# Attention in batches of two pairs of heads: where scores, turns and values stand between the weight chunks

## The chip, the cores and the metric

The kernel runs on one core of one Trainium2 chip. The metric is the device time of one execution in microseconds (us), and of several runs the median. The engines are named as in the profile: PE is TensorE (PEld is its loading of weights), DVE is VectorE, ACT is ScalarE, POOL is GpSimd, and SP's queue issues the loads of weights.

## The reference

The program is a stack of transformer layers over 256 tokens of width 1024: two layers of a first kind, then four of a second kind. The change touches only the attention of the second kind, which stands in three places: mixer "a" (layers 0 and 3) and mixer "c" (layer 2). Layer 1 has a mixer without attention. Everything is computed in 32-bit floats.

```python
def second_block(x, ...):                      # cut
    for i in range(4):
        x = x + 0.5 * rms_norm_2(swiglu(rms_norm_2(x, g[0]), ...), g[1])
        h = rms_norm_2(x, g[2])
        m = (mixer_a, mixer_b, mixer_c)[i % 3](h, ...)
        x = x + rms_norm_2(m, g[3])
        x = x + 0.5 * rms_norm_2(swiglu(rms_norm_2(x, g[4]), ...), g[5])

# mixer_a: 16 heads of width 64; a band of 64-token chunks, with a learned bias by distance
    s = einsum('bqhd,bkhd->bhqk', qc, kb) * scale + bias
    p = softmax(where(valid, s, NEG_INF));  o = einsum('bhqk,bkhd->bqhd', p, vb);  return o @ w_o
# mixer_c: 8 heads, each with two score maps of width 64 and values of width 128
    s = einsum('bqhmd,bkhmd->bmhqk', qblk, k) * scale + alibi
    p = softmax(where(allowed, s, NEG_INF)); a = p[:, 0] - lam_full * p[:, 1]
    o = einsum('bhqk,bkhe->bqhe', a, v);  return (rms_norm_2(o, subln_g) * (1 - lambda_init)) @ w_o
```

## The kernel before

**Products in three parts.** Weights arrive from memory in chunks of 1 MB (128 partitions by 2048 numbers). ACT rounds a chunk to `whi` (`Scalar.split`, shown as L1315 `whi<-raw`), DVE takes the rest to `wlo` (L1899 `wlo<-raw,whi`), and PE multiplies `whi`, `wlo` with the activations, which are split in the same way. So a product is three matmuls. Five chunks have room at once (`SLOTS`), and the split that stands at step c is that of chunk c+3 (`AHEAD`). SP loads chunk c once PE is done with chunk c-5.

**An attention stage** has 12 chunks for the queries, keys and values (`ATTEND`: v v q k q k q k q k v v) of 48 matmuls each, and then 4 blocks of the output weights. The last three blocks are multiplied in `edge`, for one half of one tile of tokens after the other. The product of a chunk goes to one of three PSUM banks in turn (0, 1, 2), and DVE takes it out with the factor of the norm (L2138 for q and k, L2142 for v).

**The eight pairs.** The heads are worked on in eight pairs, b = 0 to 7 (in "c" a pair is one head with its two maps). Each pair has the same steps: PE makes the scores (`scores`, L998 and L1000), DVE adds the bias and finds the maximum (`mask`, L2320), ACT takes the exponentials (`exps`), DVE multiplies by the reciprocals of the sums (`weigh`, L2328 and L2333; in "c" L2337 to L2343, which also mix the two maps), PE transposes the probabilities (`turn_probs`, L1013), ACT copies them out of PSUM (`keep_turned`, `prob_t<-ps`), PE multiplies them with the values (`values`, L1031 and L1033; in "c" L1025 to L1027), and DVE keeps the result (`keep_out`, L2357; in "c" L2354, after ACT's squares for the norm, `square_out`). `prob` and `prob_t` have two buffers, for even and odd b. Scores stand in banks 4 and 5, transposed probabilities in 6 and 7, and the result of one pair in bank 3.

**The order** is written out by hand, and all engines walk it in step: the scores of pairs 0, 2, 4, 6 stand in the middle of chunks 5, 7, 9, 11, those of pairs 1, 3, 5, 7 at the end of the same chunks. A pair is turned at the end of the next chunk (even b) or the one after it (odd b), and its values come one chunk later. The values of pairs 5, 6, 7 and the turns of 6 and 7 come after chunk 11, in `attend_end`. There, in "a", three of the four quarters of the first output block (`out_part`, L911 `whi,hi_first`: 6 matmuls each) fill the gaps. The fourth quarter has to wait for bank 3, so it comes when pair 7 has been kept. Output block n of "a" takes the features of pairs 2n and 2n+1, which ACT and DVE split as well (`pairs_hi`, `pairs_lo`, L2186). In "c" the result is normed first (POOL finds the factor, `scale_out` L2376 applies it), transposed by PE (`turn_attended`, L653) and split (`spot_hi`, `spot_lo` L2104). The transposes of the first half stand between the values of pairs 5 and 6.

The kernel's functions that the change touches follow.

## Time and profile before

| What | us |
| --- | --- |
| median of three runs | 2595.43 |
| the three runs | 2595.39, 2599.72, 2595.43 |
| span of the profiled execution, first to last instruction | 2589.7 |
| median of the runs less that span | 5.7 |
| PE busy | 2560.5 (99%) |
| DVE busy | 1687.8 (65%) |
| ACT busy | 1322.3 (51%) |
| share of the mean 16 DMA engines in the large queue | 58.0% |

The profiled execution has no time of its own beside the span; the runs are shown as they were timed. The granted clock of PE is 0.999 of full speed over the span. A matmul of 256 columns is listed with some 0.28 us, but one starts 0.117 us after the other, so starts are to be compared, not durations. Idle time that a row shows in brackets ends at that start and begins at the modelled end of the matmul ahead.

### The profile page before, as it was taken

Reading aid. Unit: us, or ns where it says so; the run is one execution under the profiler, and the core shown is the slowest. Engines: PE = TensorE matmul, PEld = TensorE weight load, DVE = VectorE, ACT = ScalarE, POOL = GpSimd, SP = SyncE. Lnnn points to the kernel's source line nnn. Section 1 sums busy time; section 2 is a strip of 40 time slices with the busy share of each in tenths; the row PEclk is TensorE's granted clock in tenths of the full one; section 3 lists DMA queues with packets and bytes.
Section 4 is the critical chain, followed back from the end, with each engine's and each line's share of the span. In section 5 each row is a group of like instructions: output and inputs, shape, how many; then the busy total and the mean of one; then the engine's idle time right before and its main releaser. Section 6 shows DMA issues by size and latency. Waiting matters only on the chain.

```text
span 2589.7 us, 43298 instructions
## 1 busy us (share of the span) xinstructions
PE 2560.5 (99%) x18489; PEld 2376.5 (92%) x18489; DVE 1687.8 (65%) x2365; ACT 1322.3 (51%) x1938; POOL 158.0 (6%) x228
## 2 busy tenths in 40 slices
PE   9999999999999999999999999999999999999998
PEld 8999898998998989989988998998899899897997
DVE  7778577885664766656556765656776566566663
ACT  7766376663543554444455444444554354355542
POOL 2110011000000000000011000002000000000000
PEclk9999999999999999999999999999999999999999
DMA  7267452764766546666665766756467566563863
GB/s 227 95 182 209 158 163 82 196 195 158 209 195 207 176 131 194 189 179 193 190 212 149 200 184 183 196 182 195 142 159 192 193 178 191 196 202 100 217 189 120
DMA packets 568313, 460.26 MB, mean 178 GB/s; under 512 B 10298, under 2 KB 529290, under 8 KB 568122
## 3 DMA queue, kind: packets, MB, share of 16 engines
q1 hardware_dynamic: 562615, 441.91, 58.0%
q0 software_dynamic: 4656, 15.30, 1.8%
q8 instruction: 146, 2.39, 0.4%
q14 instruction: 45, 0.37, 0.0%
q10 hardware_dynamic: 851, 0.28, 0.0%
HBM read 456.37 MB, written 1.10 MB: 177 GB/s over the span
## 4 chain that ended last, share of the span: by engine, by line
PE 90%; DVE 5%; ACT 3%; DMA 1%; issue 1%; POOL 0%; SPq 0%; DVEq 0%; POOLq 0%; ACTq 0%
PE ps L911 28%; PE ps L776 16%; PE ps L778 16%; PE ps L777 16%; PE ps L730 3%; PE ps L732 3%; PE ps L731 3%; DVE wlo L1899 1%; ACT h_hi L1315 1%; PE ps L653 1%; ACT prob L1315 1%; DVE h_lo L1961 1%; ACT whi L1315 1%; DMA raw<-in_w_in 1%; PE ps L1013 1%
## 5 line engine op out<-in xcount | busy, mean ns | idle before, releaser
L1899 DVE TENSOR_TENSOR wlo<-raw,whi 128x2048 fp32r<-128x2048 f32 (+1 forms) x419 | 957.4, 2287 | 495.4 <-ACT whi L1315 495.1
L1315 ACT ACTIVATE whi<-raw 128x2048 fp32r<-128x2048 f32 (+2 forms) x421 | 802.7, 1910 | 790.2 <-DMA raw<-in_ff_w_in 418.1
L776 PE MATMUL ps<-h_hi,whi 128*128 128x256 f32 x3584 | 1005.7, 281 | 0.0
L778 PE MATMUL ps<-h_hi,wlo 128*128 128x256 f32 x3584 | 1002.5, 280 | 0.0
L777 PE MATMUL ps<-h_lo,whi 128*128 128x256 f32 x3584 | 1001.8, 280 | 0.0
L776 PEld LDWEIGHTS ps<-h_hi,whi 128*128 128x128 f32 x3584 | 673.9, 188 | 5.0 <-issue 5.0
L778 PEld LDWEIGHTS ps<-h_hi,wlo 128*128 128x128 f32 x3584 | 674.4, 188 | 0.0
L777 PEld LDWEIGHTS ps<-h_lo,whi 128*128 128x128 f32 x3584 | 673.5, 188 | 0.0
L911 PE MATMUL ps<-whi,hid_lo 128*128 128x512 f32 x880 | 296.3, 396 | 0.0
L911 PE MATMUL ps<-whi,hid_hi 128*128 128x512 f32 x880 | 295.4, 394 | 0.0
L911 PE MATMUL ps<-wlo,hid_hi 128*128 128x512 f32 x880 | 294.6, 394 | 0.0
L730 PE MATMUL ps<-whi,h_hi 128*128 128x256 f32 (+2 forms) x992 | 284.1, 286 | 5.8 <-DVE h_lo L1961 3.6
L732 PE MATMUL ps<-whi,h_lo 128*128 128x256 f32 (+2 forms) x992 | 277.7, 280 | 0.0
L731 PE MATMUL ps<-wlo,h_hi 128*128 128x256 f32 (+2 forms) x992 | 277.6, 280 | 0.0
L2251 DVE TENSOR_TENSOR u<-ps,rb 128x512 f32<-128x512 f32 x160 | 110.5, 690 | 154.7 <-PE ps L778 154.4
L911 PEld LDWEIGHTS ps<-whi,hid_lo 128*128 128x128 f32 x880 | 165.2, 188 | 39.2
L730 PEld LDWEIGHTS ps<-whi,h_hi 128*128 128x128 f32 x992 | 188.3, 190 | 13.1 <-DVE h_lo L1961 6.2
L911 PEld LDWEIGHTS ps<-wlo,hid_hi 128*128 128x128 f32 x880 | 165.1, 188 | 38.2
L911 PEld LDWEIGHTS ps<-whi,hid_hi 128*128 128x128 f32 x880 | 165.4, 189 | 37.9
L731 PEld LDWEIGHTS ps<-wlo,h_hi 128*128 128x128 f32 x992 | 188.7, 190 | 0.7
L732 PEld LDWEIGHTS ps<-whi,h_lo 128*128 128x128 f32 x992 | 187.2, 189 | 0.0
L1315 ACT ACTIVATE h_hi<-ps,cols 128x128 fp32r<-128x128 f32 x256 | 69.6, 388 | 67.8 <-PE ps L653 67.8
(315 smaller groups left out, 2142.8 us busy)
## 6 DMA issues: line engine op xcount, KB each, us to landing
raw<-in_ff_w_in SPq DMA_DIRECT2D x176, 1024.0 KB, 6.0
raw<-in_ff_w_out SPq DMA_DIRECT2D x88, 1024.0 KB, 4.9
raw<-in_ffn_w_in SPq DMA_DIRECT2D x44, 1024.0 KB, 6.1
raw<-in_a_w_qkv SPq DMA_DIRECT2D x24, 1024.0 KB, 5.2
raw<-in_ffn_w_out SPq DMA_DIRECT2D x22, 1024.0 KB, 4.9
raw<-in_w_in SPq DMA_DIRECT2D x18, 1024.0 KB, 6.1
raw<-in_c_w_qkv SPq DMA_DIRECT2D x12, 1024.0 KB, 5.3
raw<-in_w_out SPq DMA_DIRECT2D x8, 1024.0 KB, 4.9
```

The lines of the kernel that those rows point to most:

```text
L653: ins = e.transpose(m.ps[:, 4 + n, k * P:(k + 1) * P], a[:, t, f * P:(f + 1) * P], m.ident)
L730: e.matmul(out, hi, w_hi, start=(k == 0), stop=False)
L731: e.matmul(out, hi, w_lo, start=False, stop=False)
L732: self.last = e.matmul(out, lo, w_hi, start=False, stop=(k == KT - 1))
L776: e.matmul(out, hi, m.h_hi[:, k, :], start=(k == 0), stop=False)
L777: e.matmul(out, hi, m.h_lo[:, k, :], start=False, stop=False)
L778: ins = e.matmul(out, lo, m.h_hi[:, k, :], start=False, stop=(k == KT - 1))
L911: self.last = e.matmul(m.ps[:, base + 2 * t + h, :], x, w[:, k, h * 512:(h + 1) * 512], start=(first and k == 0 and n == 0), stop=(last an ...
L1013: ins = e.transpose(m.ps[:, m.turn_bank[kind] + h, j * P:(j + 1) * P], m.prob[:, b % 2, h, j * P:(j + 1) * P], m.ident)
L1315: return self.nc.scalar.activation(*a, **k)
L1899: self.e.tensor_tensor(chunk_view(m.wlo[:, slot, :], c), chunk_view(m.raw[:, slot, :], c), chunk_view(m.whi[:, slot, :], c).bitcast(F32), ...
L2251: e.tensor_tensor(m.u[:, b % RING, :, :], view(bank, a=2), m.rb[:, :].unsqueeze(1).to_broadcast([P, 2, SEQ]), ALU.mult).then_inc(s.bank_fr ...
```

## The change

The pairs are taken in four batches of two (0 and 1, 2 and 3, 4 and 5, 6 and 7).

- Both scores of a batch stand in the middle of chunks 4, 6, 8, 10. Pair 0 of a batch uses banks 4 and 5, the other 6 and 7.
- Both turns stand at the end of chunks 5, 7, 9, 11, in the banks of the scores ("a") or in 6 and 7 ("c").
- Both values stand in the middle of chunks 6, 8, 11, ahead of the next scores; those of pairs 6 and 7 come in `attend_end`. Both results are in bank 3, and DVE keeps them with one copy of 512 columns (in "c" with two instructions of 256).
- DVE no longer splits at steps 4, 6, 8 and 10 but, together with the next, around the eviction at 5, 7, 9 and in `attend_end`.
- After chunk 11, "a" has two quarters of the output block ahead of the last values and two behind them. "c" has two groups of transposes ahead of them and all four quarters behind.

```diff
@@ class Program @@
         for c in range(12):
             self.attend_chunk(kind, l, c)
             self.attend_pairs(kind, c)
-        for c in range(12, values_at(7) + 1):
-            self.attend_pairs(kind, c)
+        self.attend_end(kind)
...
-def scores_at(b):
-    return (5, 7, 9, 11)[b // 2]
-
-
-def turned_at(b):
-    return scores_at(b) + 1 + b % 2
-
-
-def values_at(b):
-    return turned_at(b) + 1
+SCORES_AT = (4, 6, 8, 10)
+TURNED_AT = (5, 7, 9, 11)
+VALUES_AT = (6, 8, 11)
...
+def batch_of(places, c):
+    return (2 * places.index(c), 2 * places.index(c) + 1) if c in places else ()
@@ class Tensor @@
-        pair = [b for b in (0, 2, 4, 6) if scores_at(b) == c]
-        between = (lambda: self.pair_scores(kind, pair[0])) if pair else None
+        def halfway():
+            if c in VALUES_AT:
+                self.batch_values(kind, VALUES_AT.index(c))
+            if c in SCORES_AT:
+                self.batch_scores(kind, SCORES_AT.index(c))
+        between = halfway if c in VALUES_AT or c in SCORES_AT else None
...
     def attend_pairs(self, kind, c):
-        if c >= 12:
-            self.attend_end(kind, c)
-            return
-        for b in range(8):
-            if values_at(b) == c:
-                self.pair_values(kind, b)
-        for b in range(8):
-            if turned_at(b) == c:
-                self.turn_probs(kind, b)
-        for b in range(1, 8, 2):
-            if scores_at(b) == c:
-                self.pair_scores(kind, b)
...
+        if c in TURNED_AT:
+            self.batch_turns(kind, TURNED_AT.index(c))
+
+    def attend_end(self, kind):
+        if kind == "a":
+            self.out_part(kind, 0, 0)
+            self.out_part(kind, 0, 1)
+            self.batch_values(kind, 3)
+            self.out_part(kind, 1, 0)
         else:
...
+            self.round("turn")
+            self.round("attended")
+            self.turn_attended(0)
+            self.turn_attended(1)
+            self.batch_values(kind, 3)
+            self.out_part(kind, 0, 0)
+            self.out_part(kind, 0, 1)
+            self.out_part(kind, 1, 0)
+        self.out_part(kind, 1, 1)
+        self.last.then_inc(self.s.chunk_done, 1)
...
+        if (t, half) == (1, 1):
+            self.e.wait_ge(self.s.out_kept, self.p0 + 8)
+        else:
+            self.e.wait_ge(self.s.bank_free, self.b0 + 10 + 2 * t + half)
...
+    def batch_scores(self, kind, j):
+        e, m, s = self.e, self.m, self.s
+        q, k, _ = m.heads[kind]
+        e.wait_ge(s.bank_free, self.b0 + made_at("k", 2 * j) + 1)
+        self.at(s.turned_copied, self.p0 + 2 * j)
+        for b in (2 * j, 2 * j + 1):
+            bank = m.score_bank[b % 2]
...
+    def batch_turns(self, kind, j):
+        e, m, s = self.e, self.m, self.s
+        e.wait_ge(s.masked, self.p0 - 4 * self.rounds["mixers"] + 2 * j + 2)
+        for b in (2 * j, 2 * j + 1):
+            if kind == "c":
+                e.wait_ge(s.mixed, self.m0 + b + 1)
+            else:
+                e.wait_ge(s.shares, self.a0 + b + 1)
...
+    def batch_values(self, kind, j):
+        e, m, s = self.e, self.m, self.s
+        v, bank = m.heads[kind][2], m.out_bank
+        e.wait_ge(s.bank_free, self.b0 + made_at("v", 2 * j) + 1)
+        e.wait_ge(s.turned_copied, self.p0 + 2 * j + 2)
+        self.at(s.out_kept, self.p0 + 2 * j)
+        for b in (2 * j, 2 * j + 1):
...
+        ins.then_inc(s.pair_out, 2)
@@ class Scalar @@
+        if kind == "c":
+            for b in batch_of(VALUES_AT, c):
                 self.square_out(b)
+        for b in batch_of(SCORES_AT, c):
+            self.exps(kind, b)
         if kind == "a" and c == 10:
             self.pairs_hi(0)
...
+    def attend_pairs(self, kind, c):
+        for b in batch_of(TURNED_AT, c):
+            self.keep_turned(kind, b)
+
+    def attend_end(self, kind):
+        if kind == "a":
+            self.pairs_hi(1)
+            self.pairs_hi(2)
+        else:
             self.round("turn")
+            self.spot_hi("attended", 0)
+            self.spot_hi("attended", 1)
+            self.square_out(6)
+            self.square_out(7)
@@ class Vector, attend_chunk @@
+        if c < SCORES_AT[0]:
             self.split(c, 0)
         if c == 2 and kind == "c":
             self.mixing_factor()
+        if c == SCORES_AT[0]:
             e.wait_ge(s.bias_ready, self.round("bias"))
+        if c in VALUES_AT[0:2]:
+            self.keep_outs(kind, VALUES_AT.index(c))
+        for b in batch_of(SCORES_AT, c):
+            self.mask(kind, b)
+        if c in TURNED_AT:
+            b0, b1 = batch_of(TURNED_AT, c)
+            self.weigh(kind, b0)
+            if c == VALUES_AT[2] and kind == "a":
+                self.keep_outs(kind, 2)
+            self.weigh(kind, b1)
+            if c == VALUES_AT[2] and kind == "a":
+                self.pairs_lo(0)
+            elif c == VALUES_AT[2]:
+                self.keep_outs(kind, 2)
+            else:
+                self.split(c - 1, 0)
+        self.keep_chunk(kind, c)
+        if c in TURNED_AT[0:3]:
+            self.split(c, 0)
+        if (kind, c) == ("c", 9):
             self.scale_out(0)
...
+    def attend_end(self, kind):
+        if kind == "a":
+            self.split(10, 0)
+            self.pairs_lo(1)
+            self.pairs_lo(2)
+            self.keep_outs(kind, 3)
+            self.split(11, 0)
         else:
+            self.round("turn")
+            self.spot_lo("attended", 0, 0)
+            self.spot_lo("attended", 1, 0)
+            self.split(10, 0)
+            self.keep_outs(kind, 3)
+            self.split(11, 0)
@@ class Memory of banks @@
-        m.score_bank = {"a": 4, "c": 4}
-        m.turn_bank = {"a": 6, "c": 6}
-        m.out_bank = {"a": 3, "c": 3}
+        m.score_bank = (4, 6)
+        m.turn_bank = {"a": (4, 6), "c": (6, 7)}
+        m.out_bank = 3
```

The matmuls, and their number, are the same. The order on PE in an "a" stage, in the middle of the attention. Before, at the end of chunk 7: L1031 and L1033 are values, L1013 a turn, L998 and L1000 scores, L776 to L778 the product of chunks.

```order
L777 MATMUL ps<-h_lo,whi 128x256
L778 MATMUL ps<-h_hi,wlo 128x256
L1031 MATMUL ps<-prob_t,v 64x256 x2
L1033 MATMUL ps<-prob_t,v 64x128 x2
L1013 MATMUL ps<-consts,prob 128x128 x6
L998 MATMUL ps<-qk 128x128 x2
L1000 MATMUL ps<-qk 128x256 x2
L776 MATMUL ps<-h_hi,whi 128x256
L777 MATMUL ps<-h_lo,whi 128x256
```

The changed kernel, in the middle of chunk 6. L1012 and L1014 are values, L974 and L976 scores.

```order
L777 MATMUL ps<-h_hi,wlo 128x256
L1012 MATMUL ps<-prob_t,v 64x256 x2
L1014 MATMUL ps<-prob_t,v 64x128 x2
L1012 MATMUL ps<-prob_t,v 64x256 x2
L1014 MATMUL ps<-prob_t,v 64x128 x2
L974 MATMUL ps<-qk 128x128 x2
L976 MATMUL ps<-qk 128x256 x2
L974 MATMUL ps<-qk 128x128 x2
L976 MATMUL ps<-qk 128x256 x2
L775 MATMUL ps<-h_hi,whi 128x256
L776 MATMUL ps<-h_lo,whi 128x256
```

Values, turn and scores of three different pairs stood together; now values of two pairs and scores of two pairs stand together, and the turns stand alone at the ends of chunks.

The order on DVE at the end of an "a" stage. Before, from the keeping of pair 5 to the last split of an output block (L2328 and L2333 are `weigh`, L2357 keeps a pair, L2186 is `pairs_lo`, L1899 splits a chunk):

```order
L2357 COPY xn<-ps 128x256 [waits recips,pair_out]
L2328 RECIPROCAL rsum<-sums 128x4 [waits out_kept,exps]
L2333 TENSOR_SCALAR prob<-prob,rsum 128x128 [waits recips]
L2333 TENSOR_SCALAR prob<-prob,rsum 128x256
L2333 TENSOR_SCALAR prob<-prob,rsum 128x128
L2333 TENSOR_SCALAR prob<-prob,rsum 128x256
L2357 COPY xn<-ps 128x256 [waits recips,pair_out]
L2186 TENSOR_TENSOR h_lo<-xn,h_hi 128x512 [waits hi_pairs]
L2357 COPY xn<-ps 128x256 [waits recips,pair_out]
L2186 TENSOR_TENSOR h_lo<-xn,h_hi 128x512 [waits hi_pairs]
L1899 TENSOR_TENSOR wlo<-raw,whi 128x2048 [waits split_hi]
```

The changed kernel from the last `weigh` on (L2286; L2140 is `pairs_lo`, L2113 takes chunk 11 out, L2313 keeps two pairs, L1853 splits):

```order
L2286 TENSOR_SCALAR prob<-prob,rsum 128x128
L2286 TENSOR_SCALAR prob<-prob,rsum 128x256
L2140 TENSOR_TENSOR lo_first<-xn,hi_first 128x512 [waits hi_pairs]
L2113 TENSOR_SCALAR v<-ps,rs 128x256 [waits chunk_done]
L2113 TENSOR_SCALAR v<-ps,rs 128x256
L1853 TENSOR_TENSOR wlo<-raw,whi 128x2048 [waits split_hi]
L2140 TENSOR_TENSOR h_lo<-xn,h_hi 128x512 [waits hi_pairs] x2
L2313 COPY xn<-ps 128x512 [waits pair_out]
L1853 TENSOR_TENSOR wlo<-raw,whi 128x2048 [waits split_hi]
L2140 TENSOR_TENSOR h_lo<-xn,h_hi 128x512 [waits hi_pairs]
L1853 TENSOR_TENSOR wlo<-raw,whi 128x2048 [waits split_hi]
```

The two `weigh` have moved ahead of the end of chunk 11, and two splits have moved behind it.

The order on DVE at the end of the "c" stage. Before, from the keeping of pair 6 on (L2354 keeps a pair, L2104 is `spot_lo`, L1899 splits a chunk, L2376 is `scale_out`):

```order
L2354 SCALAR_TENSOR_TENSOR xn<-ps,sub_g 128x2x128 [waits sub_sq,recips,pair_out]
L2104 TENSOR_TENSOR h_lo<-ps,h_hi 128x4x128 [waits hi_turned] x2
L2354 SCALAR_TENSOR_TENSOR xn<-ps,sub_g 128x2x128 [waits sub_sq,recips,pair_out]
L1899 TENSOR_TENSOR wlo<-raw,whi 128x2048 [waits split_hi]
L2376 TENSOR_TENSOR xn<-xn,st 128x512 [waits out_kept,sub_rstd]
L2376 TENSOR_TENSOR xn<-xn,st 128x512
L2104 TENSOR_TENSOR h_lo<-ps,h_hi 128x4x128 [waits hi_turned] x2
L1899 TENSOR_TENSOR wlo<-raw,whi 128x2048 [waits split_hi]
```

The changed kernel, from the taking out of chunk 11 on (L2113; L2310 keeps, L2058 is `spot_lo`, L1853 splits, L2323 is `scale_out`):

```order
L2113 TENSOR_SCALAR v<-ps,rs 128x256 [waits chunk_done]
L2113 TENSOR_SCALAR v<-ps,rs 128x256
L2058 TENSOR_TENSOR h_lo<-ps,h_hi 128x4x128 [waits hi_turned] x2
L1853 TENSOR_TENSOR wlo<-raw,whi 128x2048 [waits split_hi]
L2310 SCALAR_TENSOR_TENSOR xn<-ps,sub_g 128x256 [waits sub_sq,pair_out]
L2310 SCALAR_TENSOR_TENSOR xn<-ps,sub_g 128x256
L1853 TENSOR_TENSOR wlo<-raw,whi 128x2048 [waits split_hi]
L2323 TENSOR_TENSOR xn<-xn,st 128x512 [waits out_kept,sub_rstd]
L2323 TENSOR_TENSOR xn<-xn,st 128x512
L2058 TENSOR_TENSOR h_lo<-ps,h_hi 128x4x128 [waits hi_turned] x2
L1853 TENSOR_TENSOR wlo<-raw,whi 128x2048 [waits split_hi]
```

One more split now stands ahead of the last keeping. The first two `spot_lo` stand ahead of it, and the split of the last output block still stands behind the last two.

## Rows read from the trace of the kernel before

**Rows 1.** The page, busy time of each engine over the span.
```profile
PE 2560.5 (99%) x18489; PEld 2376.5 (92%) x18489; DVE 1687.8 (65%) x2365; ACT 1322.3 (51%) x1938; POOL 158.0 (6%) x228
```

**Rows 2.** Windows: us, busy PE, PEld, DVE, ACT, POOL, clock, DMA share.
```profile
2348.60:2380.80 32.20, 29.79 (x215) 24.19 (x213) 21.03 (x61) 18.20 (x37) 0.00 (x0) 1.00 0.32 104
1853.60:1886.90 33.30, 29.93 (x209) 25.50 (x207) 25.35 (x70) 21.02 (x65) 5.18 (x4) 1.00 0.34 109
```

**Rows 3.** PE timeline, first "a" stage (start, us, engine, line, what).
```profile
867.27 0.28 PE L778 MATMUL ps<-h_hi,wlo 128*128 128x256 f32 x1
867.48 0.49 PE L998 MATMUL ps<-qk 64*128 64x128 f32 x4
...
868.56 0.28 PE L777 MATMUL ps<-h_lo,whi 128*128 128x256 f32 x1
868.68 0.28 PE L778 MATMUL ps<-h_hi,wlo 128*128 128x256 f32 x1
...
877.84 0.28 PE L778 MATMUL ps<-h_hi,wlo 128*128 128x256 f32 x1
...
878.74 0.28 PE L777 MATMUL ps<-h_lo,whi 128*128 128x256 f32 x1
...
893.50 0.28 PE L778 MATMUL ps<-h_hi,wlo 128*128 128x256 f32 x1
...
895.35 0.28 PE L777 MATMUL ps<-h_lo,whi 128*128 128x256 f32 x1
```

**Rows 4.** PE timeline, end of the second "a" stage.
```profile
2364.38 0.49 PE L998 MATMUL ps<-qk 64*128 64x128 f32 x4
...
2368.34 0.87 PE L1013 MATMUL ps<-consts,prob 128*128 128x128 f32 x6 [0.45 <-DVE prob L2333]
...
2374.59 0.65 PE L1031 MATMUL ps<-prob_t,v 128*64 128x256 f32 x4 [0.95 <-issue]
...
2375.98 0.51 PE L911 MATMUL ps<-whi,hi_first 128*128 128x512 f32 x1 [0.52 <-DVE xn L2357]
...
2380.78 0.50 PE L911 MATMUL ps<-whi,h_hi 128*128 128x512 f32 x1 [0.38 <-DVE wlo L1899]
```

**Rows 5.** PE timeline, the "c" stage.
```profile
1843.93 0.38 PE L1025 MATMUL ps<-v,prob_t 128*128 128x128 f32 x2
...
1844.59 0.49 PE L1013 MATMUL ps<-consts,prob 128*128 128x128 f32 x3
...
1844.84 0.37 PE L776 MATMUL ps<-h_hi,whi 128*128 128x256 f32 x1
...
1868.14 0.49 PE L998 MATMUL ps<-qk 64*128 64x128 f32 x4
...
1876.48 0.48 PE L911 MATMUL ps<-whi,h_hi 128*128 128x512 f32 x1
...
1886.88 0.50 PE L911 MATMUL ps<-whi,h_hi 128*128 128x512 f32 x1 [0.61 <-DVE wlo L1899]
```

**Rows 6.** Groups on DVE, 2337 to 2365 us (count, busy, mean ns, idle).
```profile
L1899 DVE TENSOR_TENSOR wlo<-raw,whi 128x2048 fp32r<-128x2048 f32 x4 | 9.2, 2292 | 5.8 <-ACT whi L1315 5.8
L2320 DVE CUSTOM_DVE_ANT_0 prob<-ps,bias 128x256 f32<-128x256 f32 x6 | 2.5, 418 | 0.0
L2333 DVE TENSOR_SCALAR prob<-prob,rsum 128x256 f32<-128x256 f32 x6 | 2.1, 346 | 0.0
...
L2138 DVE SCALAR_TENSOR_TENSOR qk<-ps,rb 128x512 f32<-128x512 f32 x2 | 1.4, 688 | 0.6 <-PE ps L778 0.6
```

**Rows 7.** Groups on ACT, same stretch.
```profile
L1315 ACT ACTIVATE whi<-raw 128x2048 fp32r<-128x2048 f32 x4 | 7.6, 1903 | 0.0
L1315 ACT ACTIVATE prob_t<-ps 128x768 f32<-128x768 f32 x4 | 3.2, 806 | 5.4 <-PE ps L1013 5.4
L1315 ACT ACTIVATE prob<-prob,negmax 128x256 f32<-128x256 f32 x6 | 3.0, 494 | 0.0
```

**Rows 8.** DVE timeline, first "a" stage: chunk 3 is taken out.
```profile
859.16 0.69 DVE L2138 SCALAR_TENSOR_TENSOR qk<-ps,rb 128x512 f32<-128x512 f32 x1 [1.24 <-PE ps L778]
```

More of the change, by code:

```diff
@@ L931, in blocks @@
         n = len(order) - STAGED
[L932 removed]
+        for b in range(1 if self.what in ("a_o", "c_o") else 0, n):
             for t in range(TT):
[L934 to L941 removed]
+                self.wait_block(b, t)
+                self.block(self.c0 + b, 2 * order[b], t, range(2), b == 0, False)
                 if self.what == "b_o" and (b, t) == (0, 0):
@@ L990, in edge @@
         self.head(lambda: self.turn_tile(1, scaled), after[0])
-    def scores(self, kind, b):
+    def batch_scores(self, kind, j):
         e, m, s = self.e, self.m, self.s
-        (q, k, _), bank = m.heads[kind], m.score_bank[kind]
-        self.at(s.masked, self.p0 - 4 * self.rounds["mixers"] + b)
-        for h in range(2):
-            e.matmul(m.ps[:, bank + h, 0:P], q(b, h, 0), k(b, h, 1), start=True, stop=True)
-        for h in range(2):
-            ins = e.matmul(m.ps[:, bank + h, P:P + SEQ], q(b, h, 1), k(b, h, 2), start=True, stop=True)
-        ins.then_inc(s.scores, 1)
@@ L1036, in attention @@
-    def attention(self, kind, n):
-        self.scores(kind, 0)
-        for b in range(n):
-            if b < n - 1:
-                self.scores(kind, b + 1)
-            self.turn_probs(kind, b)
-            self.values(kind, b)
-        self.p0 += n
+        q, k, _ = m.heads[kind]
[3 more added lines that the diff above has]
+            bank = m.score_bank[b % 2]
+            for h in range(2):
+                e.matmul(m.ps[:, bank + h, 0:P], q(b, h, 0), k(b, h, 1), start=True, stop=True)
+            for h in range(2):
+                ins = e.matmul(m.ps[:, bank + h, P:P + SEQ], q(b, h, 1), k(b, h, 2), start=True, stop=True)
+            ins.then_inc(s.scores, 1)
@@ new lines, in batch_values @@
+    def batch_values(self, kind, j):
+        e, m, s = self.e, self.m, self.s
+        v, bank = m.heads[kind][2], m.out_bank
[4 more added lines that the diff above has]
+            if kind == "c":
+                pt = m.prob_t[:, b % 2, 0, :]
+                t0, t1 = (m.ps[:, bank, t * SEQ + b % 2 * P:t * SEQ + b % 2 * P + P] for t in range(TT))
+                e.matmul(t0, pt[:, 0:P], v(b, 0, 0), start=True, stop=True)
+                e.matmul(t1, pt[:, P:2 * P], v(b, 0, 0), start=True, stop=False)
+                ins = e.matmul(t1, pt[:, 2 * P:3 * P], v(b, 0, 1), start=False, stop=True)
+            else:
+                out = m.ps[:, bank, b % 2 * SEQ:b % 2 * SEQ + SEQ]
+                heads = [(out[64 * h:64 * h + 64, :], m.prob_t[:, b % 2, h, :], h) for h in range(2)]
+                for to, pt, h in heads:
+                    e.matmul(to, v(b, h, 0), pt[:, 0:SEQ], start=True, stop=True)
+                for to, pt, h in heads:
+                    ins = e.matmul(to[:, P:SEQ], v(b, h, 1), pt[:, SEQ:SEQ + P], start=False, stop=True, skip_group_check=True)
+        ins.then_inc(s.pair_out, 2)
```

195 lines of the change are left out of this document (29 added, 166 removed).

## The prediction

> **What bounds the kernel now.** I read the page first: PE is busy for 2560.5 us of a span of 2589.7, in no other engine's shadow [rows 1]. So only two things can move the time: what PE does at its seams (where small matmuls interrupt the stream of chunks), and where PE waits. The windows come next. The stretch from the start of chunk 10 to the third output block holds 32.2 us in the second "a" stage, of which PE works 29.79, and 33.3 in "c" with 29.93 [rows 2]: some 2.4 and 3.4 us idle in each, in a kernel that has 29 in all. Last, the timeline of PE gives each wait its place. The middle of a stage shows none; all lie behind chunk 11, where the chain of a single pair (weigh, turn, copy, values, keep) has too little beside it [rows 4, 5].
>
> **Seams.** Chunk products of 256 columns start 0.12 us apart (868.56, 868.68), so two steps are 0.24 [rows 3]. Scores alone take from 867.27 to 868.56, less two steps: 1.05 us. A turn alone takes 877.84 to 878.74, less two steps: 0.66. Values with a turn take 893.50 to 895.35, less two: 1.61, so values take 0.95. The first score starts 0.21 after the matmul ahead, 0.09 later than a step. The first matmul behind small ones is as slow again; I take 0.10. In "a", four visits to scores and four to values go away, at 0.19 each: 1.5 us. Four visits to turns lose only their way out, 0.08 each: 0.3. That makes 1.8 a stage. In "c" the values use the whole array, so four visits to scores bring 0.8 and the rest 0.3: 1.1. Over two "a" and one "c": **4.7 us**. Nothing in the trace shows two scores together; the ends are 0 (the second pays the switch anew) and 6 (turns too are spared 0.19). I take the middle because the way in is seen on each visit.
>
> The trace shows 0.09 us for the way in, less than the rest of a matmul in the array (0.28 listed less a step of 0.12: 0.16). The Trainium skill, "TensorEngine Tiling (Array Packing)", section Key Properties, says that changing the tiling mode drains TensorE. By a full drain each way the 20 visits of scores and values that go away (eight in each "a", four in "c") would bring 6.4 us, not 3.8; the trace's 0.09 stands, and the rule only says why there should be something.
>
> **The end of an "a" stage, before.** From pair 7's scores (2364.38) to the fourth quarter (2375.98) are 11.60 us [rows 4]. Work in it: scores 1.05, three values 2.85, two turns 1.32, three quarters of 6 matmuls of 512 columns, each two steps or 0.234, 4.2 together: 9.4. So 2.2 us are waits. The brackets show 0.45 for pair 6's weights, 0.95 for pair 7's copy, 0.52 for the keeping of bank 3, each short by the modelled tail of the matmul ahead. The third block then waits for its split: 2380.78 less 2375.98 is 4.8 for 18 matmuls of 4.2, so 0.6.
>
> **The end of an "a" stage, changed.** Call the end of chunk 11 T. The scores of pairs 6 and 7 end half a chunk into chunk 10, so up to T there are 24 + 48 matmuls (8.4 us) and two values (1.8), 10.2 in all. In it DVE has two masks (four instructions of at most 0.42 each: 3.4), two weighs (four of at most 0.35: 2.8), two evictions and a keeping of 512 columns (0.69 each: 2.1) and one split of features (0.7): 9.0 at most [rows 6]. ACT's four exponentials of the second pair (at most 0.49 each and their reads, about 1.7) lie beside DVE's work [rows 7]. The keeping of pairs 4 and 5 is queued ahead of pair 7's weigh and can't begin before the middle of chunk 11 has passed: from there it takes 0.7 + 1.2 + 0.3 for semaphores, within 2.8. So the turns at T wait for nothing. They take 1.3; ACT's two copies (0.81 each) are done at T + 2.6. PE has two quarters (2.8) ahead of the values, so reaches them at T + 4.1. Values to T + 5.9, call that E. DVE has a split (2.3), two feature parts (1.4) and the eviction (0.9) until T + 4.8 and keeps the pairs by E + 0.8; PE has a quarter of 1.4 in front of the fourth. No wait either. The third block comes at E + 5.6 (four parts of 1.4). DVE goes on with a split (to E + 3.1), the last features (E + 3.8) and the third block's split (E + 6.1): wait 0.5, against 0.6. Gain 2.2 + 0.1 and the seams' 1.8: 4.1 a stage, **8.2** for both.
>
> **The end of "c".** Before, from pair 7's scores (1868.14) to the output block (1876.48) are 8.34 us. Work: scores 1.05, three values of 0.66 (1843.93 to 1844.59), two turns of 0.25 (to 1844.84), eight transposes at that pace, 0.7: 4.2 [rows 5]. So 4.1 of waits. Then 10.4 to the third block, with 36 matmuls (8.4), eight transposes and their seams (1.0): 1.0 of waits. Changed: T is again the end of chunk 11. Turns to T + 0.6, transposes of the first half to T + 1.4. ACT's copies are half as wide (about 0.5 each) and done at T + 1.4, so the values wait about 0.1 and end at E = T + 2.8; the first features are ready then. All four quarters follow, 5.6 us. Meanwhile DVE works through two feature parts, a split, the last keeping, another split and the scaling (0.7 + 0.7 + 2.3 + 0.7 + 2.3 + 0.7, from T + 2.0): the first scaled tile is there at T + 9.4, PE asks at T + 8.4 and waits 1.0. Here is what is late next: ACT's split of the third block is queued behind the last `spot_hi`, then needs 1.9 on ACT and 2.3 on DVE [rows 6, 7], plus 0.6 and latencies: 5 us from the last transposes. PE had 18 matmuls (4.2) there; the fourth quarter has moved away, 12 (2.8) are left: a wait of 2.2. Sum of waits 3.3, against 5.1: 1.8, with the seams 1.1: **2.9**.
>
> **In the middle** nothing should wait, yet cover gets thinner. From a batch's scores to its turns 8.4 us remain, for about 6 to 7 of DVE (in "c" also ACT's squares, since the keeping stands ahead of the masks). The values come half a chunk (2.8) behind the turns, and two copies need 1.6 and a latency. The first scores come in the middle of chunk 4 and need chunk 3, which was out at 859.16 + 0.69, some 1.9 us ahead of that place [rows 8]. Splits move later by a chunk but were due a chunk and more ahead. One keeping of two pairs instead of two saves DVE some 0.1 us (0.69 for a row of 512), which nobody waits for. SP's loads hang on the ends of chunks, in the same order.
>
> **Sum.** 8.2 + 2.9 = 11.1 us off a profiled span of 2589.7, 5.7 short of the runs' median. What is gained here is passed on, since the rest of PE's stream follows it and SP loads relative to it: 2595.4 - 11.1 = **2584.3 us**.
>
> **Rivals.**
> 1. The seams give nothing: scores of the second pair pay the switch anew. For: no row shows such a sequence. Against: each of the visits in rows 3 shows the way in. 2595.4 - 6.4 = 2589.0.
> 2. The ends keep a wait: DVE reaches pair 7's weigh or the last keeping late, since the splits of two blocks have moved behind chunk 11 and one stands directly ahead of the last keeping. One split of 2.3 us in the way costs, less the slack of 0.8 (turns) to 0.6 (fourth quarter), some 1.6 in each of three stages: 2595.4 - 6.3 = 2589.1.
> 3. Slower: the turns wait in every batch. Between scores and turns stand DVE (3.4 + 0.7 + 0.7 + 2.8 at most) and ACT (3.4). If they don't overlap because the two pairs go in step, the chain is 11 us against 8.4. That is a wait of up to 2.6 at each of 12 turns. From 0.9 us on (11.1 / 12) the kernel is slower; at 1.5 it is 2595.4 - 11.1 + 18 = 2602.3. Against: ACT starts on the first pair when DVE has masked it, and DVE's durations here are upper ends.
> 4. More: the seams bring 6 and the waits in "c" come out smaller by 1: 2595.4 - 11.1 - 1.3 - 1.0 = 2582.0. It is the upper end of the forecast, not a case of its own.
>
> **How the numbers follow.** Forecast 70%, with a range of its own from 2581 to 2587; rival 1 10%; rival 2 13%; rival 3 7%. What this measurement can tell from no change is 0.2%, or 5.2 us: faster means below 2590.2. The forecast, rival 1 and most of rival 2 lie there: 0.88. Rival 2 with twice the price, and rival 3 with 0.6 to 1.4 us a turn, lie within: 0.07. The rest is slower: 0.05. The range holds the forecast and both rivals at 2589, so 2580.5 to 2590.
>
> **What would show it.** In the changed profile's PE timeline: no bracket at the turns behind chunk 11, nor at the last values and the fourth quarter of "a"; two scores together at about 1.9 us; in "c" a bracket of about 2 us at the third output block and one below 1 at the second group of transposes. PE's busy time should fall by some 4 us with as many instructions less overhead, the span by 11. It would be wrong if brackets stand at L1012 (values, for `prob_t`), or at L990 (turns, for `prob`) in chunks 5 to 9, or if the first scores in chunk 4 wait for DVE.

## The result, and the profile after

The changed kernel takes **2579.28 us** (median of 5 executions, 2577.22 to 2582.46), the kernel before 2595.39 beside it (5 executions): a ratio of 0.994, 95% interval 0.9929 to 0.9951. It is faster, by 16.1 us, where I had forecast 11.1; 2579.28 lies 1.2 us below the low end of my range. The direction and the places were right, the size was not.

The page after, with the busy time that answers to [rows 1]:

```profile
PE 2553.7 (99%) x18489; PEld 2379.7 (92%) x18489; DVE 1684.9 (65%) x2357; ACT 1320.3 (51%) x1938; POOL 153.5 (6%) x228
```

PE has the same 18489 matmuls and is busy 6.8 us less; I had expected some 4. The windows after, from the start of chunk 10 to the third output block, of the second "a" stage and of "c" (us, busy PE, PEld, DVE, ACT, POOL, clock, DMA share, GB/s):

```profile
2342.80:2369.14 26.34, 26.24 (x196) 22.46 (x194) 18.55 (x41) 15.68 (x28) 0.00 (x0) 1.00 0.43 132
1851.17:1880.61 29.44, 27.15 (x197) 24.14 (x194) 23.26 (x51) 17.19 (x44) 2.58 (x2) 1.00 0.48 144
```

The windows hold other seams than those of [rows 2], so only what PE idles in them compares: 0.10 us in "a" where 2.4 had been, 2.29 in "c" where 3.4 had been. The timeline of PE at the seams of the second "a" stage (start, us, engine, line), as [rows 3] before:

```profile
2309.88 0.28 PE L777 MATMUL ps<-h_hi,wlo 128*128 128x256 f32 x1
2310.00 1.47 PE L990 MATMUL ps<-consts,prob 128*128 128x128 f32 x12
2311.23 0.37 PE L775 MATMUL ps<-h_hi,whi 128*128 128x256 f32 x1
2311.43 0.28 PE L776 MATMUL ps<-h_lo,whi 128*128 128x256 f32 x1
...
2314.04 0.28 PE L777 MATMUL ps<-h_hi,wlo 128*128 128x256 f32 x1
...
2317.44 0.28 PE L776 MATMUL ps<-h_lo,whi 128*128 128x256 f32 x1
...
2345.59 0.28 PE L731 MATMUL ps<-whi,h_lo 128*128 128x256 f32 x1
2345.80 0.49 PE L974 MATMUL ps<-qk 64*128 64x128 f32 x4
2346.13 0.60 PE L976 MATMUL ps<-qk 64*128 64x256 f32 x4
2346.56 0.39 PE L974 MATMUL ps<-qk 64*128 64x128 f32 x4
2346.78 0.60 PE L976 MATMUL ps<-qk 64*128 64x256 f32 x4
2347.32 0.38 PE L729 MATMUL ps<-whi,h_hi 128*128 128x256 f32 x1
2347.54 0.28 PE L730 MATMUL ps<-wlo,h_hi 128*128 128x256 f32 x1
...
2352.96 0.28 PE L731 MATMUL ps<-whi,h_lo 128*128 128x256 f32 x1
...
2354.84 0.28 PE L730 MATMUL ps<-wlo,h_hi 128*128 128x256 f32 x1
```

The way of reading is that of [rows 3]: from the last product ahead to the second behind, less two steps (0.23). Two pairs' scores take 1.95 less 0.23, 1.72; one pair's took 1.05, so together they save 0.39. Two pairs' values take 1.65, twice 0.95 before. Two pairs' turns take 1.32, twice 0.66: turns save nothing. Where values of two pairs stand directly ahead of scores of two pairs, as in the middle of chunk 6 (2314.04 to 2317.44), both take 3.40 less 0.23, 3.17, and not 1.65 and 1.72, 3.37: another 0.20 saved, at two places in each "a" stage. The end of the same stage, which answers to [rows 4]:

```profile
2357.55 1.47 PE L990 MATMUL ps<-consts,prob 128*128 128x128 f32 x12
2358.78 0.48 PE L889 MATMUL ps<-whi,hi_first 128*128 128x512 f32 x1
...
2361.75 0.65 PE L1012 MATMUL ps<-prob_t,v 128*64 128x256 f32 x4
...
2363.20 0.50 PE L889 MATMUL ps<-whi,hi_first 128*128 128x512 f32 x1
...
2368.64 0.40 PE L889 MATMUL ps<-whi,h_lo 128*128 128x512 f32 x1
2369.14 0.50 PE L889 MATMUL ps<-whi,h_hi 128*128 128x512 f32 x1
```

All brackets of [rows 4] are gone. The third block starts 0.50 behind the matmul ahead, a step is 0.23, so 0.27 of wait is left. The end of "c", as [rows 5]:

```profile
1866.27 1.04 PE L652 MATMUL ps<-consts,xn 128*128 128x128 f32 x8
...
1874.54 1.26 PE L652 MATMUL ps<-consts,xn 128*128 128x128 f32 x8 [0.28 <-DVE xn L2323]
...
1880.61 0.50 PE L889 MATMUL ps<-whi,h_hi 128*128 128x512 f32 x1 [2.01 <-DVE wlo L1853]
```

Start to start (the brackets are short by the modelled tail of a matmul) the second transposes wait 0.45 and the third block 2.18.

**Stage by stage.** The attention stages can be cut out of any trace: from PE's first `ps<-diag,consts` matmul in the stage to its next transposes of `x`. Executions of one kernel agree in these lengths to 0.1 us, where TensorE's clock stays up, so they measure what the runs' times (spread over 5 us) can't. Lengths in us of every trace of this study:

| kernel | first "a" | "c" | second "a" | sum |
|---|---|---|---|---|
| before | 93.62 | 92.91 | 93.56 | 280.09 |
| before again (e1) | 93.65 | 95.32 * | 93.65 | 282.62 |
| after | 88.09 | 89.04 | 88.09 | 265.22 |
| after again (e5) | 88.09 | 90.60 * | 88.10 | 266.79 |
| after, third (e11) | 88.08 | 90.59 * | 88.10 | 266.77 |
| scores apart (e2) | 89.49 | 92.13 * | 89.50 | 271.12 |
| values apart (e3) | 89.50 | 93.82 * | 89.50 | 272.82 |
| turns apart (e4) | 88.12 | 91.04 * | 88.12 | 267.28 |
| all apart (e8) | 91.81 | 91.08 | 91.74 | 274.63 |
| values early (e6) | 88.81 | 89.00 | 88.82 | 266.63 |
| split early (e7) | 88.09 | 87.86 | 88.10 | 264.05 |
| split between (e9) | 88.09 | 87.24 | 88.09 | 263.42 |
| wait filled (e10) | 88.09 | 89.02 | 88.08 | 265.19 |
| filled again (e12) | 88.09 | 89.10 | 88.08 | 265.27 |

A star marks a stretch at the lower level of TensorE's clock inside the stage: 2.4 us lost in e1, 1.5 in each of the others. The change takes 5.5 us off each "a" stage and 3.9 off "c", **14.9** in all. The rest of the program (span less the three) is 2309.6 us in the first trace of before and 2312.9 in that of after; over all fourteen traces it lies between 2309 and 2313 for either kernel. That is variation between executions, and it hid 3.3 us of the gain when the two first spans were compared (2589.7 to 2578.1, 11.6). Not all of it is the lower clock: between the markers at 967.18 and 1156.12 of the first trace of after, outside the attention, TensorE took 188.94 us, in e5 188.12 and in e11 189.16 for the same work, with a granted clock of 1.00 in all three. What slows it there stays open.

### The profile page after: what moved, and what is told of

It is laid out like the page before. It is cut to its first block, busy times and chain, and to the rows that moved or that the text cites. A ratio compares the mean times of both kernels' runs of the same rounds, so it can differ in the third digit from the quotient of the medians.

```text
span 2578.1 us, 43225 instructions
## 1 busy us (share of the span) xinstructions
PE 2553.7 (99%) x18489; PEld 2379.7 (92%) x18489; DVE 1684.9 (65%) x2357; ACT 1320.3 (51%) x1938; POOL 153.5 (6%) x228
## 4 chain that ended last, share of the span: by engine, by line
PE 92%; DVE 4%; ACT 2%; DMA 1%; issue 0%; POOL 0%; SPq 0%; DVEq 0%; POOLq 0%; ACTq 0%
PE ps L889 28%; PE ps L775 16%; PE ps L777 16%; PE ps L776 16%; PE ps L729 4%; PE ps L731 3%; PE ps L730 3%; DVE wlo L1853 1%; ACT h_hi L1287 1%; PE ps L652 1%; DVE h_lo L1915 1%; DMA raw<-in_w_in 1%; PE ps L990 0%; PE ps L976 0%; DVE xc L2497 0%
## 5 line engine op out<-in xcount | busy, mean ns | idle before, releaser
L1853 DVE TENSOR_TENSOR wlo<-raw,whi 128x2048 fp32r<-128x2048 f32 (+1 forms) x419 | 957.3, 2287 | 468.3 <-ACT whi L1287 468.0
L776 PE MATMUL ps<-h_lo,whi 128*128 128x256 f32 x3584 | 1002.8, 280 | 0.0
L776 PEld LDWEIGHTS ps<-h_lo,whi 128*128 128x128 f32 x3584 | 673.5, 188 | 0.0
L1287 ACT ACTIVATE silu<-u 128x256 f32<-128x256 f32 x204 | 82.2, 403 | 43.2 <-DVE u L2205 35.8
```

The costliest lines, as they stand in the source:

```text
L776: e.matmul(out, hi, m.h_lo[:, k, :], start=False, stop=False)
L1287: return self.nc.scalar.activation(*a, **k)
L1853: self.e.tensor_tensor(chunk_view(m.wlo[:, slot, :], c), chunk_view(m.raw[:, slot, :], c), chunk_view(m.whi[:, slot, :], c).bitcast(F32), ...
```

## Experiments

**Does a trace repeat, and does the change cost anything outside the stages? (e1, e5)** The two kernels as they are, profiled once more.

> The kernel before, profiled once more, to learn how far two traces of one kernel agree. If the +3.3 us by which the trace after is longer outside the three attention stages (+2.4 of it in the first mixing layer, up to 135 us) is variation between executions and has nothing to do with the change, this trace moves by 1 to 3 us in the same place against the first one of the same kernel, and the length of each attention stage agrees with the first trace's to within 0.3 us. The rival, that the change itself costs time outside the stages: this trace agrees with the first one everywhere to within 0.5 us.

Time 2596.24. The two "a" stages repeated to 0.1 us. Up to 135 us this trace stayed within 0.5 us of the first (0.48 later at 17 us, 0.14 at 42 us and at 89), so the place that I named was wrong. But "c" was 2.4 us longer, against my 0.3. PE's timeline of e1 at the end of "c":

```profile
1876.35 0.86 PE L1013 MATMUL ps<-consts,prob 128*128 128x128 f32 x3 [0.38 <-DVE prob L2343]
...
1879.68 0.63 PE L911 MATMUL ps<-wlo,h_hi 128*128 128x512 f32 x1
1880.11 0.63 PE L911 MATMUL ps<-whi,h_lo 128*128 128x512 f32 x1
```

The products start 0.43 apart, not 0.23. The window over them says why, and so does that of the first trace of before over the same matmuls (first e1, then before):

```profile
1879.11:1883.10 3.99, 3.99 (x12) 3.12 (x12) 2.84 (x3) 0.63 (x4) 1.85 (x2) 0.50 0.02 4
```

```profile
1876.48:1880.81 4.33, 4.33 (x22) 3.28 (x20) 3.73 (x5) 0.63 (x4) 1.86 (x2) 1.00 0.02 4
```

The granted clock is 0.50, the lower level (1.2 GHz), in e1, and 1.00 in before, for the same work. It fell after PE had stopped three times within 3 us (ahead of 1873.88, 1875.06 and 1876.35 of its timeline, 0.4 to 0.6 each), waiting for DVE's weights and ACT's copies. The first trace of before has the same stops (ahead of 1872.17, 1873.35 and 1874.64) and no fall. The first trace of after lost 2.4 us at the start against that of before. Of these 1.1 are a longer wait (2.31 for ACT's `proj`, ahead of 36.83, where before has 1.17 at the same place), and the other 1.3 are of the same kind as in e1, since the window there has 0.57:

```profile
36.00:40.00 4.00, 3.17 (x15) 3.20 (x16) 3.19 (x7) 3.93 (x5) 0.00 (x0) 0.57 0.81 268
```

> The changed kernel, profiled once more. Two claims are tried. First, the stages are fixed: the three attention stages are as long as in the first trace of it, to within 0.1 us, but for stretches at the lower level of TensorE's clock. Second, what differs between executions is only such stretches: the first trace had one at 36 to 40 us (granted clock 0.53 to 0.61, 2.4 us lost) that the trace of before had not, and no other ahead of the last 5 us. If that belongs to the execution and not to the change, this trace has it elsewhere or not at all, and its span is then 2575.4 to 2577.5. If the change causes it, it is at 36 to 40 us again.

Time 2579.55, span 2577.8. No stretch at 36 to 40 us (granted clock 1.00): it belonged to that execution. Both "a" stages repeated to 0.01 us. The span came out 0.3 above what I gave, since a stretch of 1.5 us stood in another place, right behind the third block's wait. PE's timeline there and the window:

```profile
1875.91 0.40 PE L889 MATMUL ps<-whi,h_lo 128*128 128x512 f32 x1
1878.33 0.50 PE L889 MATMUL ps<-whi,h_hi 128*128 128x512 f32 x1 [2.01 <-DVE wlo L1853]
...
1879.71 0.63 PE L889 MATMUL ps<-wlo,h_hi 128*128 128x512 f32 x1
1880.14 0.63 PE L889 MATMUL ps<-whi,h_lo 128*128 128x512 f32 x1
```

```profile
1878.00:1882.00 4.00, 3.67 (x10) 2.91 (x11) 2.94 (x3) 1.19 (x3) 0.00 (x0) 0.61 0.00 0
```

**What is a seam worth? (e2, e3, e4)** A visit is one interruption of the chunk products by small matmuls, and their form is the part of the array that they use (64 rows for scores, 64 columns for values in "a", all of it for turns). In the changed kernel the second pair of every batch moves 12 products further, once for the scores, once for the values, once for the turns. The edit for the scores:

```
        def halfway():
            ...
            if c in SCORES_AT:
-               self.batch_scores(kind, SCORES_AT.index(c))
+               self.batch_scores(kind, SCORES_AT.index(c), (0,))
+       def later():                      # called before product 4 of the second half
+           if c in SCORES_AT:
+               self.batch_scores(kind, SCORES_AT.index(c), (1,))
```

> The second pair's scores of every batch stand 12 products later, on their own: 12 more visits to the 64-row form, nothing else moved. Theory A (each visit to the 64-row form costs TensorE some 0.38 us, so the merging of visits is what the change brings): +1.5 us in each of the three attention stages, +4.6 us in all, 2583.9. Theory B (the gain came from the ends of the stages, where waits went, and visits cost nothing): 0, 2579.3. In the trace by A each visit of two pairs' scores (1.72 us behind its last product) becomes two of 1.05.

2582.62 (4 executions), +1.4 in each "a" stage, +1.6 in "c" before its stretch at the lower clock: +4.4, of which I had expected 4.6. A visit of one pair is 1.29 less 0.23, 1.05:

```profile
2347.93 0.28 PE L731 MATMUL ps<-whi,h_lo 128*128 128x256 f32 x1
2348.14 0.49 PE L988 MATMUL ps<-qk 64*128 64x128 f32 x4
...
2349.22 0.28 PE L730 MATMUL ps<-wlo,h_hi 128*128 128x256 f32 x1
```

Theory A holds: a further visit to the scores' form costs 0.35 to 0.39.

> The values of a batch's second pair stand 12 products later, on their own; at the end of an "a" stage they stand one quarter of the output product later. By theory A each extra visit costs 0.25 us where the values are written 64 columns at a time ("a"), so +1.0 us in each "a" stage, and nothing where all 128 columns are used ("c"): +2.0 in all, 2581.3. By theory B 0. If the keep of the last two pairs comes too late, the third block of the output product in "a" waits some tenths more; that shows at its place.

2584.24 (4 executions), +1.4 in each "a" (I had 1.0: a pair's values alone take 1.00, so two visits cost 0.35 more than a merged one) and +3.2 in "c", where I had 0. The theory of the visits holds there too (values of one pair take 0.67, of two together 1.34), but turns began to wait. PE's timeline of e3 in "c", and one piece of DVE's:

```profile
1835.50 0.52 PE L1005 MATMUL ps<-consts,prob 128*128 128x128 f32 x3
1837.16 0.55 PE L1005 MATMUL ps<-consts,prob 128*128 128x128 f32 x3 [1.15 <-DVE prob L2312]
```

```profile
1829.87 0.76 DVE L2326 SCALAR_TENSOR_TENSOR xn<-ps,sub_g 128x256 f32<-128x256 f32 x2 [6.21 <-ACT sub_x L1303]
1830.55 0.28 DVE L2290 CUSTOM_DVE_ANT_0 prob<-ps,bias 128x128 f32<-128x128 f32 x1
```

The turns wait for DVE's weights, here and again at 1853.78: each of these two visits takes 2.30 where 0.66 is its work, 1.6 more, and that is all of the 3.2. The delay comes through DVE's queue: the keeping of both pairs (1829.87) waits for ACT's squares of the second pair's values, and the masks of the next batch stand behind the keeping (1830.55). The second pair's values stand some 3.1 us later than in the changed kernel (behind two scores and 12 products), and the second pair's turn waits 1.3. It is my rival 3 (turns that wait in the middle), not in the changed kernel but one step beside it: the cover in "c" is some 1.8 us.

> The turns of a batch's second pair stand 12 products later, on their own; at the end of the stages they stand behind a quarter of the output product ("a") or the first of the transposes ("c"). Turns use the whole array: both theories say that the visit alone costs nothing (0.665 us for six turns, 1.32 for twelve), so 0 to +0.3 us and 2579.3 to 2579.6. If every change of what is computed costs TensorE a fixed time, whatever its form (theory C), it is +0.25 to +0.38 a visit, 12 visits: +3.0 to +4.6.

2580.79 (4 executions), +0.03 in each "a" stage for four more visits. A full-array visit costs nothing, and theory C (any change of work costs) is out. In "c" it is +0.5 without the stretch at the lower clock, nearly all at one place: the last values (1865.62 of its timeline) come 0.44 later, since they wait for ACT's copy of the last turned tile, which ends at 1865.51. That is a wait at the end and not a price of the visits: each of the six split visits in the middle takes 0.33.

**All three apart (e8)**

> Scores, turns and values of the second pair all stand apart. If the costs of the single separations add up (scores +1.4 in each "a" stage and +1.6 in "c", values +1.4 in each "a" and +3.25 in "c", of which 2.8 are two waits of turns for VectorE's weights, turns 0): +2.8 in each "a" stage, +4.8 in "c", +10.4 in all, 2589.7. What is left in "a" against the kernel before (5.5 less 2.8 = 2.7 us a stage) is then the end of the stage. Rival: separated turns give the second pair's chain room, so that the two waits in "c" shrink; then "c" is +2 to +3.5 and the whole 2587 to 2588.5.

2588.75 (10 executions; ratio to before 0.9982, 0.9973 to 0.9991). +3.7 in each "a" stage, +2.0 in "c", 9.4 in all. "c" went as the rival said: the waits of e3 in the middle are gone when the turns are apart too. In "a" it is 0.9 more than the sum of the parts, mostly from one place, a wait of 0.95 at the last values (at 2368.37 of its timeline). With the seams of the kernel before, or nearly so, the order of the changed kernel still keeps 280.1 less 274.6, 5.5 us: that comes from the ends of the stages.

**What do the ends bring? (e6)**

```
         if kind == "a":
+            self.batch_values(kind, 3)
             self.out_part(kind, 0, 0)
             self.out_part(kind, 0, 1)
-            self.batch_values(kind, 3)
             self.out_part(kind, 1, 0)
```

> At the end of an "a" stage the last batch's values stand right behind its turns, ahead of the two first quarters of the output product, which no longer hide ScalarE's copy of the turned tiles. Theory (the quarters hide that copy): TensorE waits 1.2 us for the copy (it ended at 2359.91, the turns at 2358.71), and the third block's wait of 0.27 goes since the keep comes earlier: +0.9 in each "a" stage, +1.9 in all, 2581.1. Rival (the order at the end is worth nothing, the gain of the "a" stages is all in the seams): 0, 2579.3.

2580.16 (4 executions), +0.72 and +0.73 in the "a" stages, where the theory had 0.9 and the rival 0. PE's timeline:

```profile
2354.53 1.47 PE L990 MATMUL ps<-consts,prob 128*128 128x128 f32 x12
2356.99 0.65 PE L1012 MATMUL ps<-prob_t,v 128*64 128x256 f32 x4 [0.99 <-issue]
```

So the two quarters do hide ACT's copy; moving them costs the wait and gives back a part at the third block.

**The wait that the change left (e7, e9).** ACT splits the fourth output chunk of "c" only behind its last `spot_hi`. In e7 ACT does it before (`self.split(12, 0)` behind `square_out(7)`), and DVE takes its part ahead of both second `spot_lo`; in e9 DVE takes it between them.

> In the "c" stage the weights of the fourth block of the output product are split earlier: ScalarE's part right behind its last squares (it idles there from 1870.1 to 1875.2), VectorE's part between scale_out and the low halves of the second transposes. Theory: the wait of 2.2 us ahead of the third staged block (its low weights are late) falls to 0.2 or less and the low halves are not late: -2.0 us, 2577.3; and the stretch at the lower clock that three of the traces show right behind that wait (1.5 us lost) does not come back, since TensorE no longer stops there. Rival: the low halves of the second transposes become late by as much as the split takes (2.28), and the wait only moves to them: 0 to +0.3, 2579.3 to 2579.6.

2576.36 (5 executions; ratio 0.9931, 0.9919 to 0.9944). "c" is 1.2 us shorter than in the changed kernel, between the theory (2.0) and the rival (0): the third block waits no more, but the second staged block waits for the low half, as these rows of PE and then DVE show. No stretch at the lower clock in "c".

```profile
1872.48 1.26 PE L652 MATMUL ps<-consts,xn 128*128 128x128 f32 x8 [0.26 <-DVE xn L2326]
...
1875.97 0.47 PE L889 MATMUL ps<-whi,h_hi 128*128 128x512 f32 x1 [0.84 <-DVE h_lo L2061]
```

```profile
1872.94 2.28 DVE L1854 TENSOR_TENSOR wlo<-raw,whi 128x2048 fp32r<-128x2048 f32 x1
1875.14 1.28 DVE L2061 TENSOR_TENSOR h_lo<-ps,h_hi 128x512 fp32r<-128x512 f32 x2
```

> As e7_split_early, but VectorE's split stands between the low halves of the two second transposes: token tile 0 first, whose halves TensorE wants at 1874.97 of that trace, then the split (2.28), then tile 1, which is wanted 8 us later. Theory: the wait of 1.0 ahead of the second staged block goes (its low half would be there at about 1874.45), and the third staged block, wanted at 1876.37, waits for the split's end at about 1876.75 with 0.1 behind it: 0.45. So -0.55 against e7_split_early, -1.8 against the changed kernel's undisturbed stage, 2575.8, and again no stretch at the lower clock in the "c" stage. Rival: some other producer (ScalarE's high half of tile 1) is late, and it ends as e7_split_early, 2576.4.

2576.70 (5 executions; ratio 0.9936, 0.9922 to 0.9949). "c" is 0.62 shorter than in e7 and 1.80 shorter than in the changed kernel, as expected. PE and then DVE:

```profile
1876.66 0.50 PE L889 MATMUL ps<-whi,h_hi 128*128 128x512 f32 x1 [0.21 <-DVE wlo L1854]
```

```profile
1873.72 0.69 DVE L2061 TENSOR_TENSOR h_lo<-ps,h_hi 128x512 fp32r<-128x512 f32 x1 [0.78 <-ACT h_hi L1287]
1874.33 2.28 DVE L1854 TENSOR_TENSOR wlo<-raw,whi 128x2048 fp32r<-128x2048 f32 x1
1876.52 0.68 DVE L2061 TENSOR_TENSOR h_lo<-ps,h_hi 128x512 fp32r<-128x512 f32 x1
```

Both are faster than the changed kernel: their 10 executions lie between 2575.87 and 2578.34, the 11 of the changed kernel between 2577.22 and 2584.92 (median 2579.87). By the runs' times e7 and e9 can't be told apart; by the stage e9 is the shorter.

**Is it the stop that brings the clock down? (e10, e11, e12)** The wait stays, but PE multiplies through it:

```
                 for b in range(STAGED):
+                    if self.what == "c_o" and (t, half, b) == (0, 0, STAGED - 1):
+                        self.filler(14)        # 14 products into bank 4, read by nobody
                     if half == 0:
                         self.wait_block(b, t)
```

> The changed kernel with 14 products of 256 columns, whose results nothing reads, put into the wait ahead of the third staged block of "c" (2.2 us long; they take 14 x 0.117 = 1.6), so that TensorE doesn't stop while the wait keeps its end. Theory (TensorE's stop there is what the clock falls after): the third staged block begins where it did, the stage from its first to its last marker is as long as in the first trace of the changed kernel to within 0.15 us, and the stretch at granted clock 0.5 right behind the wait (in 5 of the 7 traces that have this wait of 2.2) is not there, in the profiled run nor, by the mean clock, in the others: median 2578.0 or lower. Rival (the low stretch comes for another reason, such as the long span of lighter work before): it is there again, at 1.5 us, and the median is 2579.3 to 2579.6.

2577.96 (5 executions). (The count in the text above is wrong: it was 4 of 7 traces.) "c" has its undisturbed length, 89.02, and granted clock 1.00:

```profile
1875.06 1.84 PE L625 MATMUL ps<-whi 128*128 128x256 f32 x14
1877.24 0.50 PE L895 MATMUL ps<-whi,h_hi 128*128 128x512 f32 x1 [0.34 <-DVE wlo L1861]
```

> The changed kernel a third time, beside e12_filled_again on the same chip, to count the stretches at the lower clock: 4 of the 7 traces with the unfilled wait of 2.2 us in "c" have one right behind it (the count of 5 in the expectation of e10_wait_filled was one too many). Theory: here the median of the runs lies 0.8 to 1.5 us above that of e12_filled_again. Rival (the stretches have nothing to do with the wait): the two medians agree to 0.5 us.

> The kernel of e10_wait_filled again. Theory: no stretch at the lower clock in the "c" stage, as in its first trace, and a median 0.8 to 1.5 us below that of e11_after_third. Rival: a stretch behind the filled wait, or medians within 0.5 us.

e11, the changed kernel, took 2580.28 and has the stretch (its "c" is 90.59); e12 took 2578.11 and has none: 2.2 us apart, more than the 0.8 to 1.5 of the theory. Not all of that is the stretch: of the 2.8 us between the two profiled spans 1.5 lie in "c" and 1.3 outside the attention stages, where neither trace has a low clock before its last 3 us. Counted over all traces: with the stop of 2.2 us 5 of 8 have a stretch at the lower clock right behind it; where it is filled (e10, e12), or cut to 1.0 and 0.4 us (e7, e9), 0 of 4. Two comparisons of medians point the same way. That is support, not proof: if the share were 5 in 8, four traces without one would come by chance about once in fifty, and if that share is itself taken as uncertain (all 5 of the 12 traces' stretches falling among those 8), about once in fourteen. The filled wait alone, 0 of 2, would be chance once in seven. That the stop brings the clock down is not shown.

## Why the prediction was right and wrong

- **Direction and places: right.** No bracket at the turns behind chunk 11, at the last values or at the fourth quarter of "a"; nothing waits in the middle; in "c" the third block waits 2.18 (I had 2.2).
- **The seams: the step that failed.** The mechanism was right and its price was not. I worked out 1.8 us for an "a" stage and 1.1 for "c", 4.7 in all. All visits of one stage, measured in the two traces in the way of [rows 3], take 21.3 and 18.4 us in "a", 16.4 and 14.9 in "c": 2.9, 2.9 and 1.5, **7.3** in all. I had counted 0.19 for each visit to scores or values that goes away. It is 0.39 for scores (0.35 in e2) and, in "a", 0.25 against the kernel before or 0.35 against e3 for values. The change of form costs scores some 0.10 at four places, and I had two of them. My 0.09 for the way in was right: the first score starts 0.21 behind the matmul ahead. So was my 0.10 for the first product behind. What I left out is that the first group of small matmuls is itself slow (the first four scores take 0.33 to the next group, the same of the next pair 0.22: 2345.80 to 2346.13, 2346.56 to 2346.78), and that the last group is too (four scores of 256 columns take 0.43 ahead of other scores and 0.54 ahead of a product: 2346.13 to 2346.56, 2346.78 to 2347.32). I also left out the 0.20 where values stand directly ahead of scores, four times in the two "a" stages. And I gave 0.08 for each visit of turns that goes away, where there is nothing (e4): 0.3 too much in every stage, hidden in the sum. The ends that I gave for this term were 0 and 6; 7.3 lies outside.
- The Trainium skill, "TensorEngine Tiling (Array Packing)", Key Properties, says that changing the tiling mode drains TensorE. The runs bear out that it is the change of form that costs, since scores (64 rows) and values (64 columns) pay, and full-array turns and the full-array values of "c" don't; that a drain is what takes the time no run shows. My estimate by a full drain, 6.4 us for scores and values, where I had 3.8, was nearer to the 7.3. In part that is luck: it had 0.32 for each visit, where scores cost more and values less. I had set the rule behind the 0.09 of one row, which shows only a part of what a change costs.
- **The ends of the stages: right, a little low.** "a": 5.5 less 2.9 is 2.6 a stage, I had 2.3; the third block waits 0.27, not 0.5. "c": 3.9 less 1.5 is 2.4, I had 1.8; the second transposes wait 0.45, not 1.0, since DVE took 6.95 us from its first `spot_lo` (1867.53) to the first scaled tile, where my sum of its work had 7.4. Together 1.2 us more. e8 gives 5.5 for the same part once more against 7.6 here; the difference is its own wait of 0.95 in each "a" stage and its later values in "c". No run puts the order of before back at the end of "c" alone, so the 2.4 there rests on the rows.
- **The sum.** 14.9 measured in the stages against 11.1: 2.6 from the seams, 1.2 from the ends.
- **The base.** I took 2595.43, the median of three runs, as the time from which to subtract. Over 45 runs of that kernel in this study the median is 2593.7 (2591.7 to 2602.3), and 11 runs of the changed one give 2579.9: 13.9 apart, not 16.1. The last 1.2 us of my miss (5.0 less 3.8) is of that size. A stretch at 0.5 (1.5 to 2.4 us each) is only one part of what spreads the runs: e5 and e11 have none outside the attention stages before the last 3 us, and yet that rest takes 2311.0 and 2311.9 us, where e10's takes 2309.3.
- **Rivals.** 1 (seams give nothing) and 2 (the ends keep a wait) are refuted by e2 and by the rows of the end; 3 (turns wait in every batch) didn't come, though e3 shows how near it is in "c". Rival 4 had the right direction and was too small, 2582.0.

## What to carry to other kernels

Where PE is the bound and small matmuls of half the rows or columns stand between large ones, count the changes of form, not the small matmuls: here 0.35 to 0.39 us for each visit to scores, 0.25 to 0.35 for values, and next to none for small matmuls of the full array. Price a seam by whole visits, one against two together, never by the one gap at its start. When the last waits of PE are a chain through other engines, look at what each in-order engine does just before: moving the split of one block forward in the queues of ACT and DVE was worth 1.8 us.

## What the hardware showed that I had not expected

- **The clock fell behind short stops, though not always.** With PE busy for 99% of the span the granted clock still went to 0.50 (the lower of its two levels, 1.2 GHz) for some 3 us in 5 of 8 traces behind one stop of 2.2 us, and for some 7 us (1876.4 to 1883.3) in one of two traces behind several stops of 0.4 to 0.6. The products of 512 columns then start 0.427 us apart instead of 0.233. In e8 it also fell in layer 1, 1.0 us behind this stop:

```profile
1373.86 2.85 PE L1056 MATMUL ps<-b_uv,b_wt 128*128 128x128 f32 x16 [2.02 <-DVE b_uv L2377]
```

  The stop at that place is 1.3 us long in twelve of the other traces and 1.8 in the first of before, and none of these falls. Ahead of a trace's last microseconds the fourteen traces have nine low stretches, and each begins in a stop or within 1.6 us of its end. The Trainium skill, "TensorE: Matmul & The Clock Gate", Part 1, says that the gate is set by how busy TensorE has recently been, and that the moment at which it turns to full speed varies from run to run. The nine places agree with the first; the second is about the rise, which no run here times, and what varies here is whether the clock falls at all.
- **The lengths of the attention stages repeat to 0.1 us** in traces whose whole times differ by 3, as long as the granted clock is 1.00: comparing two traces from marker to marker resolves there what the medians of five runs can't. It doesn't hold for every part of the program (188.1 to 189.2 us between the same two markers outside the attention, above).
